# Two conditioned transformer blocks on one core: a second buffer pair for modulation blocks 8 to 15, and the closing norm's scale applied ahead of its root

## The reference, cut to what matters

```
for l in range(DEPTH):
    mod = (silu(c) @ w_ada[l] + b_ada[l])            # shifts, scales, gates: 6 x 1024
    mod_c = silu(c_ctx) @ w_ada[l] + b_ada[l]        # the same for the context
    h  = modulate(rmsnorm(x,  norm1_g[l]), sh1, sc1)
    hc = modulate(rmsnorm(xc, norm1_g[l]), csh1, csc1)
    ...                                              # conv branch, attention, gates, w_out
    x = x + g2 * conv_ffn(h2, w_up[l], ffn_dw[l], ffn_dw_b[l], w_down[l])
...
# second block, at its end
x = x + MACARON_W * g * swiglu(h, ffn_w_gu[layer, 1], ffn_w_down[layer, 1])
return rmsnorm_2(x, final_norm_g)                    # x * rsqrt(mean(x*x) + EPS) * g
```

## Time and profile before

| | us |
|---|---|
| median of 3 runs | 2342.61 |
| lowest and highest | 2340.86, 2350.02 |
| the profiled execution | 2344.2 |
| its span, first to last instruction | 2342.5 |

### The profile page before, as it was taken

One profiled execution on the slowest core, in us unless ns is written; L12 is line 12 of the kernel. 1 busy time (PEld: TensorE's weight loads), 2 busy tenths in 40 slices (PEclk: granted clock), 3 DMA queues, 4 the chain that ended last, 5 costly groups with the idle time before them and its releaser, 6 DMA issues.

```text
span 2342.5 us, 49545 instructions
## 1 busy us (share of the span) xinstructions
PE 2233.5 (95%) x18082; PEld 2148.1 (92%) x18082; DVE 1833.8 (78%) x3242; ACT 1311.7 (56%) x2145; POOL 119.9 (5%) x231
## 2 busy tenths in 40 slices
PE   7999999998999999899999999999999999989998
PEld 5888899998899999789999999998999999979998
DVE  4796867869789976987998878868877877878655
ACT  3366655526766555476664644647644644686443
POOL 0100000000000000000000001000001001000000
PEclk8999999999999999999999999999999999999999
DMA  8746676754347775444687677671678687735654
GB/s 337 240 161 210 224 237 207 256 186 146 124 154 268 265 249 172 161 136 154 215 279 256 227 275 269 212 258 64 227 274 273 211 288 260 240 121 171 230 168 129
DMA packets 150406, 499.80 MB, mean 213 GB/s; under 512 B 17392, under 2 KB 21616, under 8 KB 148720
## 3 DMA queue, kind: packets, MB, share of 16 engines
q1 hardware_dynamic: 113360, 374.01, 46.5%
q0 software_dynamic: 32544, 119.55, 16.3%
q10 hardware_dynamic: 4352, 4.20, 0.6%
HBM read 496.65 MB, written 1.05 MB: 212 GB/s over the span
## 4 chain that ended last, share of the span: by engine, by line
PE 70%; DVE 14%; ACT 7%; DMA 4%; issue 4%; ACTq 0%; DVEq 0%; SPq 0%; POOLq 0%; POOL 0%
PE bank_pair L1849 21%; PE bank_pair L1851 20%; PE bank_pair L1850 20%; DVE w_lo L1124 4%; DMA modraw<-in_w_mod 3%; DVE arena L1405 3%; ACT w_hi L600 2%; PE bank_pair L1966 1%; PE ps_o L1862 1%; DVE h_lo L1286 1%; DVE small L1480 1%; ACT arena L836 1%; DVE arena L1663 1%; ACT h_hi L685 1%; DMA e_plain<-in_w_mod 1%
## 5 line engine op out<-in xcount | busy, mean ns | idle before, releaser
L1124 DVE TENSOR_TENSOR w_lo<-raw,w_hi 128x1024 fp32r<-128x1024 f32 (+2 forms) x748 | 820.6, 1113 | 210.6 <-ACT w_hi L600 207.2
L600 ACT ACTIVATE w_hi<-raw 128x1024 fp32r<-128x1024 f32 (+2 forms) x748 | 712.5, 967 | 403.4 <-PE bank_pair L1851 263.6
L1849 PE MATMUL bank_pair<-h_hi,w_hi 128*128 128x256 f32 x2928 | 841.9, 288 | 12.5 <-DVE arena L1663 5.8
L1850 PE MATMUL bank_pair<-h_lo,w_hi 128*128 128x256 f32 x2928 | 831.7, 284 | 0.0
L1851 PE MATMUL bank_pair<-h_hi,w_lo 128*128 128x256 f32 x2928 | 831.5, 284 | 0.0
L1849 PE MATMUL bank_pair<-e_both,w_hi 128*128 128x256 f32 (+1 forms) x2064 | 592.5, 287 | 22.1 <-DVE e_both L1784 10.0
L1849 PEld LDWEIGHTS bank_pair<-h_hi,w_hi 128*128 128x128 f32 x2928 | 564.8, 193 | 34.8 <-issue 25.8
L1851 PE MATMUL bank_pair<-e_both,w_lo 128*128 128x256 f32 (+1 forms) x2064 | 586.5, 284 | 0.0
L1850 PE MATMUL bank_pair<-e_both,w_hi 128*128 128x256 f32 (+1 forms) x2064 | 586.4, 284 | 0.0
L1850 PEld LDWEIGHTS bank_pair<-h_lo,w_hi 128*128 128x128 f32 x2928 | 565.3, 193 | 0.3
L1851 PEld LDWEIGHTS bank_pair<-h_hi,w_lo 128*128 128x128 f32 x2928 | 565.0, 193 | 0.0
(11 more groups left out here) (263 smaller groups left out, 2185.3 us busy)
## 6 DMA issues: line engine op xcount, KB each, us to landing
modraw<-in_w_mod POOLq DMA_DIRECT2D x224, 512.0 KB, 5.1
raw<-in_w_gu SPq DMA_DIRECT2D x176, 512.0 KB, 4.5
raw<-in_w_up SPq DMA_DIRECT2D x132, 512.0 KB, 5.1
raw<-in_w_gate SPq DMA_DIRECT2D x48, 512.0 KB, 3.7
raw<-in_w_dn SPq DMA_DIRECT2D x64, 384.0 KB, 4.5
raw<-in_w_dn SPq DMA_DIRECT2D x64, 320.0 KB, 3.7
raw<-in_w_down SPq DMA_DIRECT2D x48, 384.0 KB, 5.4
raw<-in_w_down SPq DMA_DIRECT2D x48, 320.0 KB, 4.6
```

The source lines that it names most:

```text
L600: nc.scalar.activation(w_hi[:, p, HALF * f:HALF * f + w], raw[:, p, HALF * f:HALF * f + w], ACT.Copy)\
L1124: nc.vector.tensor_tensor(w_lo[:, p, at], raw[:, p, HALF * f:HALF * f + w], w_hi[:, p, at].bitcast(F32), ALU.subtract).then_inc(lo_ready, 1)
L1849: nc.tensor.matmul(out, l[0], r[0], start=start, stop=False)
L1850: nc.tensor.matmul(out, l[0], r[1], start=False, stop=False)
```

## The change

The change has two parts.

**Modulation blocks 9, 11, 13 and 15** get a second pair of half buffers, `mod_next`, a view of `arena`. Its first load waits until PE has used all of blocks 0 to 7, since one of their buffers lies under it; later ones wait for the block two before. Blocks 10, 12, 14 and 16 go to `modraw` and likewise wait for the block two before. From block 17 on the loads are issued as before. PE's `mods` picks the tile and the semaphore by the block's number.

**The closing norm**: each 128x256 part of `x` is multiplied by the gain into `x_gain` as soon as it is final (`final_gain`, eight new instructions, seven within the last stage and one behind the last update). After the root three broadcast multiplications, over 3, 3 and 2 parts, replace the eight of L1368, and three stores replace the two.

```
+N_TWO = 16
+Y_PARTS = (slice(0, 3), slice(3, 6), slice(6, DC))
...
+AHEAD = N_FIRST + (N_TWO - N_FIRST) // 2 - 1
...
+        x_gain = view(6144, DC, T)
...
+        mod_next = view(free0 + 2048, 2, D)
...
-            for f in range(2):
-                sp.wait_ge(norm_out, 4 * (f + 1))
-                sp.dma_start(a["y"][:, 4 * f:4 * f + 4, :], nsq[:, 4 * f:4 * f + 4, :]).then_inc(stored, 16)
-            sp.wait_ge(stored, 32)
+            for f, ks in enumerate(Y_PARTS):
+                sp.wait_ge(norm_out, f + 1)
+                sp.dma_start(a["y"][:, ks, :], nsq[:, ks, :]).then_inc(stored, 16)
+            sp.wait_ge(stored, 16 * len(Y_PARTS))
...
-            with pool.Fori(N_FIRST + 1, N_PE) as m:
+            for m in range(N_FIRST + 1, N_TWO, 2):
+                for c in range(2):
+                    pool.wait_ge(mod_mm, 2 * N_FIRST if m == N_FIRST + 1 else 2 * m - 3 + c)
+                    nc.gpsimd.dma_start(mod_next[:, c, :], a["w_mod"][m, :, D * c:D * (c + 1)])\
+                        .then_inc(mod_next_in[c], 16)
+                for c in range(2):
+                    load_mod(m + 1, c, mod_mm, 2 * m - 1 + c)
+            with pool.Fori(N_TWO + 1, N_PE) as m:
...
                         update(n["before"], k)
+                        if n["dest"] == "y":
+                            final_gain(n["before"], k)
...
                 if n["dest"] == "y":
-                    for k in range(DC):
-                        nc.vector.scalar_tensor_tensor(out=nsq[:, k, :], in0=x[:, k, :], scalar=pcol("final_b", k),
-                                                       in1=nrm[:, 3, :], op0=ALU.mult, op1=ALU.mult)\
-                            .then_inc(norm_out, 1)
+                    dve.wait_ge(x_gained, DC)
+                    for ks in Y_PARTS:
+                        m = ks.stop - ks.start
+                        nc.vector.tensor_tensor(nsq[:, ks, :], x_gain[:, ks, :],
+                                                nrm[:, 3:4, :].broadcast_to([P, m, T]), ALU.mult).then_inc(norm_out, 1)
...
+            def final_gain(s, k):
+                dve.wait_ge(updated, s.x0 + k + 1)
+                nc.vector.tensor_scalar(x_gain[:, k, :], res["x"][:, k, :],
+                                        pcol("final_b", 0, DC).unsqueeze(2)[:, k, :], None, ALU.mult)\
+                    .then_inc(x_gained, 1)
...
                                 scaled_lo(n, k)
+                            if n["dest"] == "y":
+                                final_gain(s, k)
                         split_lo(after_next(s, b, p, last), 0)
...
-                mod_rows(m, modraw, (0, 1) if s.mods == 2 else (p,), 16 * (m - N_FIRST + 1))
+                halves = (0, 1) if s.mods == 2 else (p,)
+                if s.m0 >= N_TWO:
+                    mod_rows(m, modraw, halves, 16 * (m - AHEAD))
+                elif (m - N_FIRST) % 2 == 0:
+                    mod_rows(m, modraw, halves, 16 * ((m - N_FIRST) // 2 + 1))
+                else:
+                    mod_rows(m, mod_next, halves, 16 * ((m - N_FIRST) // 2 + 1), mod_next_in)
```

More of the change, by code:

```diff
@@ L403, in build @@
         mod_in = [sem("mod_in0"), sem("mod_in1")]
+        mod_next_in = [sem("mod_next_in0"), sem("mod_next_in1")]
         mod_mm, mod_row, mod_turn, mod_done = (sem(f"mod_{k}") for k in ("mm", "row", "turn", "done"))
@@ L414, in build @@
             sem(k) for k in ("sq2_ready", "sq2_added", "sum2_ready", "log2_ready", "std2_ready"))
-        norm_out = sem("norm_out")
+        norm_out, x_gained = sem("norm_out"), sem("x_gained")
         glu_sig, glu_mul = sem("glu_sig"), sem("glu_mul")
@@ L1150, in mod_product @@
                 dve.wait_ge(c_ready, 3)
-                dve.wait_ge(mod_in[p], 16 * (m - N_FIRST + 1))
+                dve.wait_ge(mod_in[p], 16 * (m - AHEAD))
                 nc.vector.scalar_tensor_tensor(out=modraw[:, p, :], in0=modraw[:, p, :], scalar=1.0, in1=vector,
@@ L1851, in mm3, with mod_rows @@
                 return nc.tensor.matmul(out, l[1], r[0], start=False, stop=stop)
-            def mod_rows(m, tile, halves=(0, 1), arrived=None):
+            def mod_rows(m, tile, halves=(0, 1), arrived=None, came=mod_in):
                 for c in halves:
                     if arrived is not None:
-                        pe.wait_ge(mod_in[c], arrived)
+                        pe.wait_ge(came[c], arrived)
                     if c == 0:
```

## The result

| | before | after |
|---|---|---|
| median of 5 runs, us | 2342.61 | 2333.59 |
| lowest and highest, us | 2340.86, 2350.02 | 2330.31, 2334.07 |
| profiled execution (span), us | 2344.2 (2342.5) | 2334.07 (2332.4) |

A forecast was written before the change was run, and what follows sets the result against it. PE's matmuls bound the kernel, with waits for modulation loads in `q`, `k`, `v`. Gains of 11.7 (pair) and 1.1 (closing norm), 12.8 us, took the 2342.6 median to 2329.8; range 2327.0 to 2336.0.

The forecast's parts named there:

- An undisturbed cycle of 7.17 us, no wait for a load, clock at 1.00: Each of six cycles (one slab, one block) in `q`, `k`, `v` takes 7.17 us, without load waits, at full clock.
- The cover: Time to spare between a block load's landing and its use in the six cycles, about 6 us.
- 11.7 us for the pair: Six cycles in `q`, `k`, `v` shrink from 54.76 to 43.02 us through the second buffer pair.
- a third of the gain rests on the clock staying up when the gaps are gone: In the third and fifth of the six cycles, 3.8 us together were pure clock and would be gained.
- part 2: The closing norm and stores at the program's end gain 1.1 us, with bounds of 0.8 and 1.45.
- `gate` gives back up to 0.65, costed at nothing: At the start of `gate`, 0.65 us would return if DVE set the pace; costed at nothing.
- DVE's slack of 0.55: DVE's sum is ready 0.55 us a cycle before PE's next turn needs it; costed at nothing.
- The DMA engines, at nothing: In the six cycles 13.2 MB at 307 GB/s costs no time; bound 3 us given back.
- The rival: Transfers bound the six cycles at 265 GB/s; gain 7.8 us, time 2334.8; chance 0.17.
- the last store's better end: At the program's end, the smaller last store adds 0.28 us to DVE's earlier end.
- The clock later: Rival: new clock falls in later work, 2.3 us each; six more outweigh 12.8 us; clearly more falls, chance 0.04.
- the forecast's own sign of being wrong: Distance from `gate` to the span's end grown by more than 1 us would mean gain given back later.

The follow-up runs named there:

- the pair alone: Changed kernel with the closing norm and its two stores as before, keeping the second buffer pair; median 2334.84 us, ratio to before 0.9959.
- the four stores: Changed kernel with the closing multiplication and the stores in four parts of 256 KB; 2329.57 us in one run.
- the kernel with late issue: Changed kernel, but each load into the second pair waits for the block just before; `gate` began at 115.07 us, 3.7 us lost, no whole time given.
- the two first traces: Profiled executions of the kernel before and the changed kernel, nothing further changed; spans 2342.5 and 2332.4 us.
- one more instruction: Changed kernel with one idle 128x256 DVE multiplication more in each slab of `q`, `k` and `v`; 2340.82 us in all.
- the norm alone: Kernel before with only the new closing norm, one buffer pair for all blocks from 8 on; median 2342.40 us, ratio to before 0.9998.

## Why the prediction came out as it did, point by point

**An undisturbed cycle of 7.17 us, no wait for a load, clock at 1.00.** Right in all three traces of the changed kernel, and in those of the pair alone and of the four stores. The lead of the issue is the cause (the kernel with late issue). The cover was put at 6 us and was 4.5 for the slowest load; the loads of block 9 went out at 42.5 and not around 39.

**11.7 us for the pair.** Right against the one trace it was made from, and mis-sized as a gain of the median. The step that failed is "a third of the gain rests on the clock staying up when the gaps are gone": after the change it did stay up, but before the change it hadn't always been down. I took 3.8 us of falls in one execution for a property of the kernel. Four traces with one pair give 7.6 to 11.7, mean 9.7: the term was 2 us too large (1.6, if the pair's worth is counted to the start of `gate`, 10.1). With the 0.2 of part 2 this is about half of the 3.8 us by which the median was missed; the rest, which no run here takes apart, is less than the spread of the later stretch. That the 11.6 us of the two first traces met the 11.7 so closely is luck in part: another execution of before could have given 8.

**`gate` gives back up to 0.65, costed at nothing.** Right: from the end of block 15's matmuls to the first scores it is 111.89 - 107.98 = 3.91 us, and 3.92 before.

**DVE's slack of 0.55.** The cost, nothing, was right: in after the sum ends 6.6 us behind the turn and PE never waited for it. The size was read too large, since the turn began 0.15 behind the sum even where it waited for it. What could be used was 0.4, and one more instruction held the turn by 0.1.

**The DMA engines, at nothing.** Right. The rival held that the queues share 265 GB/s; they gave 249 to 332, by what was asked.

**Part 2, 1.1 us.** 0.9. DVE's end came 0.84 earlier, as reckoned (0.82). Of the last store's better end I had expected 0.28, and it was about 0.1: 256 KB landed 2.5 us behind their issue, where the 512 KB of the earlier trace rows took 2.6. The `final_gain` instructions cost nothing, at 0.35 each and not 0.41: the last stage's eight updates took 25.20 us with them and without.

**The clock later.** The forecast named it as a rival by which 2.3 us go with each new fall, and held the number of falls for fixed otherwise. The number varies from one execution to the next by as much as this rival supposed of the change. By the forecast's own sign of being wrong, a distance from `gate` to the end of the span grown by more than 1 us, the two first traces spoke against it: 2219.0 and 2220.5. But the 2.4 us that they differ by up to the last update lie within the 10 us by which executions of one kind differ, and over four and five traces the means are the same.

Not settled is what is left between the two ways of reading the result: by the ratio the gain is 11.9 us (8.7 to 15.2), by the sum of the mean terms 9.7 + 0.9 = 10.6, by the medians 9.0 in the first comparison and 2343.47 - 2332.53 = 10.9 in the second. All of them agree within what 5 or 6 runs can tell.

## What to carry to other kernels

A buffer that is asked for once a cycle needs its load issued more than a landing ahead of its use; give it a second place and move the issue, for with the place alone waits came back. Of a stretch that is long at a low clock, count as sure only what is idle, and take the rest for a cost that some executions have: look at a second trace of the same kernel before a price is put on it. Before PE's gaps are closed, measure how much idle time the next engine has left in the shortened cycle (here 0.76 us), and how far ahead of PE it delivers (0.4): one instruction more cost 0.3 us in all, four cost 5.4.

## What the runs showed of the hardware

The same program on the same input does not have its clock falls at the same places. Of three traces of the kernel before, one fell twice in the six cycles, one once there and once right behind them, and one not at all. A fall came during a gap of 1.39 us in one trace, and at a gap of 1.67 there was none in another; the length of the gap alone doesn't decide it. In none of the eight traces in which PE had no gap in these cycles did the clock fall there. Executions of the kernel before spread over 9.2, 13.4 and 13.3 us in the three comparisons (5, 18 and 11 runs), those of the norm alone over 13.5 (12 runs), those of the changed kernel over 3.8 and 5.1 (5 and 6 runs) and of the pair alone over 6.3 (7 runs). More runs make a wider range, but 9.2 and 3.8 are of five each: closing the gaps seems also to have taken out some of the spread.

Stores issued close behind each other landed by their size and by what stood in front of them. Four of 256 KB landed in 2.0 to 2.3 us each, one of 256 KB behind two of 384 KB in 2.5, and two of 512 KB in 2.6.

A wait of PE between the halves of a block costs some 0.2 us beside its idle time: 0.64 and 0.64 us of busy time in place of 1.07.
